# Padding between on-chip buffers: the addresses of x and of the gated layer against those of the weights

## The reference

```python
def swiglu(x, w_in, w_out):
    g, u = jnp.split(x @ w_in, 2, axis=-1)
    return (jax.nn.silu(g) * u) @ w_out

for layer in range(2):
    if layer == 1:
        k, v = split(rmsnorm(h, kv_norm) @ w_kv)
    h = h + 0.5 * swiglu(rmsnorm(h, ffn1_norm[layer]), ffn1_w_in[layer], ffn1_w_out[layer])
    hn = rmsnorm(h, mix_norm[layer])
    h = h + (s5_mixer(hn, ...) if layer == 0 else moba_attention(hn, w_q, w_o, k, v, ...))
    h = h + 0.5 * swiglu(rmsnorm(h, ffn2_norm[layer]), ffn2_w_in[layer], ffn2_w_out[layer])
return rmsnorm(h, final_norm)
```

## Time and profile before

| | |
|---|---|
| median of 3 runs | 1048.19 us (1046.75 to 1048.33) |
| profiled execution | 1047.26 us |
| its span, first to last instruction | 1045.5 us |
| mean granted TensorE clock | 0.965 |
| TensorE busy (matmuls) | 1008.5 us, 5680 instructions |
| VectorE, ScalarE, GpSimd busy | 610.8, 488.3, 234.7 us |
| read from memory | 167.33 MB |

### The profile page before, as it was taken

The page is one execution under the profiler, slowest core; times in us unless marked ns, Lnnn a source line. Parts: engine busy times, 40 slices in busy tenths (PEclk is TensorE's granted clock), DMA queues, the critical chain, the costliest instruction groups (busy, mean ns, idle before and its releaser), DMA issues.

```text
span 1045.5 us, 14378 instructions
## 1 busy us (share of the span) xinstructions
PE 1008.5 (96%) x5680; PEld 810.5 (78%) x5680; DVE 610.8 (58%) x756; ACT 488.3 (47%) x720; POOL 234.7 (22%) x291
## 2 busy tenths in 40 slices
PE   5999999889899999999999999999989999999996
PEld 4888888767788888888888888888855688888885
DVE  4676656798566555545655555545555465555543
ACT  6544544432455444435544444434543465444441
POOL 4999989798000000000000000000000000000000
PEclk9999999999999999999999999999975799999999
DMA  9766666500356565665556665666520155656651
GB/s 336 214 183 181 195 186 180 160 3 4 103 191 188 179 186 172 199 193 180 180 184 183 182 183 177 184 185 182 180 75 1 44 177 185 191 180 191 182 161 40
DMA packets 47890, 169.31 MB, mean 162 GB/s; under 512 B 5968, under 2 KB 5968, under 8 KB 47824
## 3 DMA queue, kind: packets, MB, share of 16 engines
q1 hardware_dynamic: 46368, 166.74, 52.5%
q10 hardware_dynamic: 1456, 1.66, 0.4%
HBM read 167.33 MB, written 1.05 MB: 161 GB/s over the span
## 4 chain that ended last, share of the span: by engine, by line
PE 92%; POOL 4%; DVE 2%; ACTq 1%; issue 0%; ACT 0%; POOLq 0%; DVEq 0%
PE ps L965 88%; PE ps L976 2%; POOL w_bd L440 2%; POOL c_bd L451 2%; PE ps L1175 1%; POOL decay L458 1%; PE ps L989 1%; PE ps L1002 0%; DVE scan L880 0%; DVE fin L958 0%; PE ps L1074 0%; DVE rot_b L887 0%; ACTq L485 0%; DVE rot_a L868 0%; ACT L603 0%
## 5 line engine op out<-in xcount | busy, mean ns | idle before, releaser
L726 DVE TENSOR_TENSOR w_lo<-raw,w_hi 128x1024 fp32r<-128x1024 f32 x312 | 405.2, 1301 | 283.2 <-ACT w_hi L501 282.6
L501 ACT ACTIVATE w_hi<-raw 128x1024 fp32r<-128x1024 f32 x312 | 329.4, 1058 | 278.0 <-PE ps L965 277.9
L965 PE MATMUL ps<-w_hi,x_hi 128*128 128x512 f32 x896 | 357.2, 399 | 11.0 <-DVE w_lo L726 11.0
L965 PE MATMUL ps<-w_hi,x_lo 128*128 128x512 f32 x896 | 352.3, 393 | 0.0
L965 PE MATMUL ps<-w_lo,x_hi 128*128 128x512 f32 x896 | 352.0, 393 | 0.0
L965 PEld LDWEIGHTS ps<-w_hi,x_hi 128*128 128x128 f32 x896 | 169.2, 189 | 46.7 <-issue 11.3
L965 PEld LDWEIGHTS ps<-w_hi,x_lo 128*128 128x128 f32 x896 | 168.9, 188 | 37.9
L965 PEld LDWEIGHTS ps<-w_lo,x_hi 128*128 128x128 f32 x896 | 169.4, 189 | 35.8
L321 POOL TENSOR_TENSOR ms<-ss 128x2 f32<-128x2 f32 x7 | 1.4, 199 | 775.5 <-ACT act_out L539 774.2
L965 PE MATMUL ps<-w_hi,hid_hi 128*128 128x512 f32 x352 | 139.4, 396 | 0.0
L965 PE MATMUL ps<-w_lo,hid_hi 128*128 128x512 f32 x352 | 138.9, 395 | 0.0
(11 more groups left out here) (113 smaller groups left out, 695.7 us busy)
## 6 DMA issues: line engine op xcount, KB each, us to landing
raw<-in_in SPq DMA_DIRECT2D x176, 512.0 KB, 3.9
raw<-in_out SPq DMA_DIRECT2D x88, 512.0 KB, 3.7
raw<-in_glu SPq DMA_DIRECT2D x16, 512.0 KB, 3.9
raw<-in_k SPq DMA_DIRECT2D x8, 512.0 KB, 4.4
raw<-in_v SPq DMA_DIRECT2D x8, 512.0 KB, 4.2
raw<-in_q SPq DMA_DIRECT2D x8, 512.0 KB, 4.4
raw<-in_o SPq DMA_DIRECT2D x8, 512.0 KB, 4.2
xt<-in_xt SPq DMA_DIRECT2D x4, 256.0 KB, 6.1
```

What stands on the lines that cost most here:

```text
L501: act.activation(w_hi[:, gu % WS, :], raw[:, gu % RAW, :], ACT.Copy)\
L726: dve.tensor_tensor(w_lo[:, gu % WS, :], raw[:, gu % RAW, :], w_hi[:, gu % WS, :].bitcast(F32), ALU.subtract)\
L965: return pe.matmul(o, w, x, start=start, stop=stop, skip_group_check=True)
```

## The change

Six pads are added between buffers, and the one there was is renamed. The distances afterwards are: `raw` and `w_hi` as before, `w_lo` 32, `x0_hi` 96, `x0_lo` 256, `hid_hi` 384, `hid_lo` 448, `x1_hi` 64, `x1_lo` 192. `h`, `prod`, `act_out` and `ident` move by 256 bytes, the second area by 320, and the tensors from `k_sb` on by 576 in all. No instruction is added, taken away or moved.

```diff
@@ -105,8 +105,11 @@
     with ctx:
         raw = sb("raw", [P, RAW, UW])
         w_hi = sb("w_hi", [P, WS, UW], F32R)
+        sb("pad0", [P, 8])
         w_lo = sb("w_lo", [P, WS, UW], F32R)
+        sb("pad1", [P, 16])
         x0_hi = sb("x0_hi", [P, DT, TOK], F32R)
+        sb("pad2", [P, 40])
         x0_lo = sb("x0_lo", [P, DT, TOK], F32R)
         h = sb("h", [P, TT, D])
         prod = sb("prod", [P, 2, TT, HB])
@@ -121,7 +124,8 @@
         mhalf = sb("mhalf", [P, TT])
         rs = sb("rs", [P, TT])
 
-        sb("pad", [P, 24])
+
+        sb("pad3", [P, 24])
 
 
         with ExitStack() as area:
@@ -135,6 +139,7 @@
             rot_a = sb("rot_a", [P, PPT, 2, CH], F32, area)
             rot_b = sb("rot_b", [P, PPT, 2, CH], F32, area)
         hid_hi = sb("hid_hi", [P, FT, TOK], F32R)
+        sb("pad4", [P, 16])
         hid_lo = sb("hid_lo", [P, FT, TOK], F32R)
 
 
@@ -152,7 +157,9 @@
             rot_in = sb("rot_in", [P, PPT, 2, CH], F32, area)
             scan = sb("scan", [P, PPT, 2, CH], F32, area)
             states = sb("states", [P, 2, PPT, 2, CH], F32, area)
+        sb("pad5", [P, 32])
         x1_hi = sb("x1_hi", [P, DT, TOK], F32R)
+        sb("pad6", [P, 32])
         x1_lo = sb("x1_lo", [P, DT, TOK], F32R)
         k_sb = sb("k_sb", [P, DT, TOK])
         v_sb = sb("v_sb", [P, TT, D])
```

## The result

The changed kernel takes 1056.89 us (median of 4 runs, 1055.14 to 1059.49), the kernel before 1048.26 us beside it. The ratio is 1.0081 with a 95% interval of 1.0054 to 1.0108: slower by 0.8%, 8.6 us, where 1.2% faster was forecast. The profiled execution is 1055.14 us with a span of 1053.4 us, 7.9 us longer than before, at nearly the same mean clock, 0.966 against 0.965. Of the four executions two had a mean clock of 0.966 and took 1055.14 and 1055.28 us and two had 0.957 and 0.959 and took 1059.49 and 1058.51 us, so the 7.9 us of the two profiled ones compare like with like better than the medians do.

A forecast was written before the change was run, and what follows sets the result against it. TensorE's matmul starts were taken as the bound, 227.5 or 233 ns apart depending on the loaded buffer's distance from the weights. 1047.3 - 6.2 (x1) - 5.4 (gated layer), all else 0, gave 1036 us, range 1020 to 1060.

The forecast's parts named there:

- the sum: Whole kernel: 1047.3 us minus 6.2 for x1 and 5.4 for the gated layer gives 1035.7, so 1036 us.
- 227.5 for all: Dense matmuls: x0, x1 and the gated layer all run at 227.5 ns per matmul at their new distances.
- The two terms: Dense matmuls: x1 gives back 6.2 us over 1152 matmuls, the gated layer 5.4 us over 1056.
- x0 loses its place: Matmuls loading x0 fall to 233 ns, the rest stays: 8.4 us more, 1055.7 us; chance 0.33.
- The distance does nothing: Dense matmuls: memory region, not distance, sets the pace, so pads change nothing: 1047 us; chance 0.13.
- Better than any seen: Dense matmuls: half of the 14 ns above the 213.3 floor goes, 220.4 ns each, 1009 us; chance 0.07.
- VectorE and ScalarE at 0: Making `w_lo` (1.30 us) and `w_hi` (1.06 us): moved addresses cost nothing, covered by the 2.7 us unit.
- Transfers at 0: DMA and SyncE queue: `raw` and packets unchanged, the queue waits 900 us for `w_lo`, so no effect.
- Mixed: Dense matmuls: x0 falls to 233 ns, the others rise to 227.5, or each lands between: 1044.1 us; chance 0.14.
- The sign: Whole kernel against no change: faster 0.48, same 0.19, slower 0.33, with 2 us as the distinguishable difference.
- The range: Whole kernel time: 1020 to 1060 us.

The follow-up runs named there:

- the map: Six kernels differing from the kernel before only in pads, one load-to-stream distance each for x0, gated layer and x1: 1059.67, 1054.05, 1050.30, 1056.30, 1045.54 and 1045.82 us.
- the first experiment: Kernel before with x1 and the gated layer moved from distance 128 to 0, so every buffer is at 0: 1036.03 us, ratio 0.989.

## Why the prediction was wrong

**The reading of the kernel before was right.** TensorE's pace between starts sets the time, the pace goes with the buffer that is loaded, and 1036.03 us with every buffer at 0 is the 1036 that the sum gives when "227.5 for all" holds. The two terms were of the right size: 11.6 us expected of x1 and the gated layer, 12.1 us measured between the two profiled executions (1047.26 and 1035.16 us, both at a mean clock of 0.965).

**The step that failed** is "I take 227.5 for all", and its reason, that 128 was more likely the unlucky place than 0 the single lucky one. It is the other way round. In the changed kernel x1 and the gated layer stayed at 233 ns and x0 rose to 232.7. In the map seven of eight steps of 32 bytes are slower than 0, six of them as slow as 128. The gaps of rows 10 were read as one pair in two that meets something extra. The alternation is there (229 and 238 ns by the starts in the trace), but it is one of several rhythms that all average 233 ns, and so no sign of a collision that belongs to 128. At 64/160/64 the changed kernel has three gaps of 0.23 to 0.24 in the place of a short and a long one, at the same mean:

```profile
350.72 0.39 PE L972 MATMUL ps<-w_hi,x_lo 128*128 128x512 f32 x1
350.96 0.39 PE L972 MATMUL ps<-w_hi,x_hi 128*128 128x512 f32 x1
351.19 0.40 PE L972 MATMUL ps<-w_lo,x_hi 128*128 128x512 f32 x1
351.43 0.40 PE L972 MATMUL ps<-w_hi,x_lo 128*128 128x512 f32 x1
```

Two values of a curve, one good and one bad, said nothing on which of them is the rule. What tipped the choice was a picture of a collision, with no row of a third distance behind it.

**The rival that came true** is "x0 loses its place": 1055.7 us expected, 1055.14 in the profiled execution and 1056.89 in the median. Its price, 8.4 us, was a little high by the paces: 11.17 us for 48 is 232.7 ns, and 1536 x 5.2 = 8.0 us. By the stages of the table x0's phases lost about 7 us. The 1.5 us of the S5 stage are no part of the rival; they lie inside what that stage varies by from trace to trace.

**The distance does nothing** (0.13) fell with the first experiment. Nor does the trace agree with the rule of the Trainium skill that stood behind it (SBUF — State Buffer, section "Who interferes with whom"; TensorE: Matmul & The Clock Gate, section "Step-by-step: what each phase is for"), that a load takes no bandwidth from the running matmul: 227.5 and 233 ns for the same program at two distances, and 215.9 once the stream stands. Whether the two reads meet at a port or in the memory behind it, no run shows. The Trainium skill's even gap for 512 columns, 215.7 ns (TensorE: Matmul & The Clock Gate, section "Wait — 56ns, not 53.3ns?"), is met by that last kernel alone.

**Better than any seen** (0.07) was right that most of the 14 ns is not the cost of changing the loaded tile, since 11.6 of them go when the stream stands, and wrong that a distance removes them: in sixteen steps of 32 bytes and three finer ones none is under 226.8 ns for a run of 48 or more.

**VectorE and ScalarE at 0**: 1307 and 1058 ns against 1301 and 1058, the first wait on `w_lo` 10.8 against 11.0 us. Right. **Transfers at 0**: the SyncE queue waits 907.6 us for `w_lo` against 899.8; right.

**Mixed** (0.14) did not come: neither x1 nor the gated layer got quicker. The six distances of its side-by-side pairs, 96, 224, 384, 416, 64 and 160, all stand in slow rows of the map.

**The sign** was forecast at 0.48 for faster against 0.33 for slower. With two settings seen and six new ones to come, nothing in the rows supported more for the one than for the other. The range reached to 1060 because of the rival, and the measured time lies in it.

What stays open: why level reads still cost 11.6 ns, why 192 is rather quick, and how the stream before and the stream after a change of weights buffer share in it. The runs give the prices. That the two reads meet in the memory is the reading that fits them, and it is not shown.

## What to carry to other kernels

When the time between two starts on TensorE is over columns / clock although nothing is awaited, compare that time between phases that load from different buffers: a steady difference of some ns can be a matter of addresses. Put the loaded tiles at a whole multiple of 256 bytes from the streamed ones (0 and 256 were measured, in this number format), both high and low parts, and let streams that follow one another share that distance too; here one pad of 480 bytes in place of 96 gave 1.1%. And where a trace shows a resource at two settings alone, a change to third ones is a coin toss: move the bad to the good one that is known before trying new ones.

## What the runs showed of the hardware that was not expected

Start-to-start times of 128x512 matmuls in this number format depend on the distance between the loaded and the streamed tile with a period of 256 bytes: 227 ns at 0, 229 at 192, 232.5 to 234 at the others of a 32-byte raster, 231 at 8. At 16 bytes the same phase shows runs of 10.90 and of 11.20 us for 48. One load in three off level raises the mean of all three by 5 to 6 ns, nearly as much as three do. A stream that stands on one column brings 215.9 ns and saves 4.5% of the kernel, and a load that stands brings 231.7.
